# Even attention: a fourth probability buffer, paired ratios, scores three units ahead and issued later in the iteration

## The reference, cut to what matters

```python
def diff_attend(q, k, v, lam):
    s = jnp.einsum('bqhmd,bkhmd->bhmqk', q, k).astype(jnp.float32) * (A_QK ** -0.5)
    p = jax.nn.softmax(s, axis=-1)
    a = p[:, :, 0] - lam * p[:, :, 1]
    return jnp.einsum('bhqk,bkhd->bqhd', a, v.astype(jnp.float32))
```

## Time and profile before

| what | us |
|---|---|
| median of 3 runs | 2271.23 (2267.19 to 2271.67) |
| the profiled execution | 2276.89 |
| its span in the profile | 2275.2 |
| PE busy | 2193.6 (96% of the span) |
| DVE busy | 1353.2 (59%) |
| ACT busy | 557.7 (25%) |
| mean granted TensorE clock | 0.976 of full |

### The profile page before, as it was taken

How to read it: one execution, slowest core, us unless ns; L and a number is a source line. 1 busy time by engine, 2 the same in 40 slices (tenths; PEclk the granted TensorE clock), 3 DMA queues, 4 the chain that set the end, 5 groups by cost and what they waited for, 6 DMA issues and landing times.

```text
span 2275.2 us, 28228 instructions
## 1 busy us (share of the span) xinstructions
PE 2193.6 (96%) x11848; PEld 1785.6 (78%) x11848; DVE 1353.2 (59%) x1761; ACT 557.7 (25%) x1088; POOL 47.8 (2%) x31
## 2 busy tenths in 40 slices
PE   8999998889899999999999999999999999999998
PEld 5788885568788767777788888788888887888887
DVE  5123447985562374766697763464787536977733
ACT  3111015871231462364321110131100002211100
POOL 0000000000000020300000000000000000000000
PEclk8899999999799999999999999999999999999999
DMA  6232233221031112202222322322222222222322
GB/s 278 116 111 111 111 115 81 67 74 56 19 140 56 39 54 75 74 20 75 74 93 95 109 78 94 107 86 99 83 85 72 91 98 93 93 93 93 112 101 74
DMA packets 34238, 204.52 MB, mean 90 GB/s; under 512 B 4800, under 2 KB 5056, under 8 KB 14656
## 3 DMA queue, kind: packets, MB, share of 16 engines
q1 hardware_dynamic: 32736, 197.99, 25.0%
q10 hardware_dynamic: 1376, 4.72, 0.6%
HBM read 191.16 MB, written 2.10 MB: 85 GB/s over the span
## 4 chain that ended last, share of the span: by engine, by line
PE 87%; DVE 9%; ACT 2%; issue 1%; DMA 0%; DVEq 0%; SPq 0%; ACTq 0%
PE ps L412 23%; PE ps L413 22%; PE ps L414 22%; PE ps L518 3%; PE ps L519 3%; PE ps L520 3%; DVE stat L2110 2%; PE ps L633 2%; PE ps L567 1%; PE ps L550 1%; PE ps L1261 1%; PE ps L966 1%; PE ps L739 1%; PE ps L614 1%; PE ps L560 1%
## 5 line engine op out<-in xcount | busy, mean ns | idle before, releaser
L1833 DVE CAST whi<-raw 128x2048 fp32r<-128x2048 f32 (+2 forms) x148 | 172.0, 1162 | 448.4 <-DMA raw<-in_even 120.0
L412 PE MATMUL ps<-h2hi,whi 128*128 128x512 f32 (+1 forms) x1052 | 412.3, 392 | 2.6 <-DVE h2lo L1933 2.2
L413 PE MATMUL ps<-h2lo,whi 128*128 128x512 f32 (+1 forms) x1052 | 407.3, 387 | 0.0
L414 PE MATMUL ps<-h2hi,wlo 128*128 128x512 f32 (+1 forms) x1052 | 407.3, 387 | 0.0
L1834 DVE TENSOR_TENSOR wlo<-raw,whi 128x2048 fp32r<-128x2048 f32 (+2 forms) x148 | 320.1, 2163 | 5.1
L412 PE MATMUL ps<-h1hi,whi 128*128 128x512 f32 (+1 forms) x768 | 273.8, 356 | 5.4 <-DVE h1lo L1880 2.6
L413 PE MATMUL ps<-h1lo,whi 128*128 128x512 f32 (+1 forms) x768 | 269.5, 351 | 0.0
L414 PE MATMUL ps<-h1hi,wlo 128*128 128x512 f32 (+1 forms) x768 | 267.5, 348 | 0.0
L412 PEld LDWEIGHTS ps<-h2hi,whi 128*128 128x128 f32 x1052 | 197.8, 188 | 49.4 <-DVE h2lo L1933 8.3
L414 PEld LDWEIGHTS ps<-h2hi,wlo 128*128 128x128 f32 x1052 | 197.8, 188 | 40.5
L413 PEld LDWEIGHTS ps<-h2lo,whi 128*128 128x128 f32 x1052 | 197.9, 188 | 38.8
(11 more groups left out here) (323 smaller groups left out, 3350.8 us busy)
## 6 DMA issues: line engine op xcount, KB each, us to landing
raw<-in_ffn_in SPq DMA_DIRECT2D x44, 1024.0 KB, 4.9
raw<-in_even SPq DMA_DIRECT2D x16, 1024.0 KB, 7.6
mod_w<-in_mod SPq DMA_DIRECT2D x6, 2048.0 KB, 20.3
mraw<-in_mod SPq DMA_DIRECT2D x12, 1024.0 KB, 4.9
raw<-in_odd SPq DMA_DIRECT2D x12, 1024.0 KB, 4.9
raw<-in_sgu_v SPq DMA_DIRECT2D x12, 1024.0 KB, 4.8
raw<-in_sgu_u SPq DMA_DIRECT2D x12, 1024.0 KB, 4.9
raw<-in_sgu_out SPq DMA_DIRECT2D x16, 768.0 KB, 4.3
```

The source lines that it names most:

```text
L412: pe.matmul(o, r(lhi), r(rhi), start=first, stop=False, **kw)
L413: pe.matmul(o, r(lhi), r(rlo), start=False, stop=False, **kw)
L414: return pe.matmul(o, r(llo), r(rhi), start=False, stop=last, **kw)
L1833: step(dve.tensor_copy(whi[:, slot, 0:width].bitcast(F32R), raw[:, slot, 0:width]))
```

## The change

Two things are done at once. There are four probability buffers instead of three (two of them now lie where the last two tiles of h1hi and the first ones of h1lo will be written, so the last two convolved_parts get a wait for the transposes of unit 44). And the queues are shifted: PE issues the scores three units ahead, and no longer at the head of the iteration but behind the late transposes and the half of the products; ACT makes the exponentials two units ahead; DVE makes the maxima three units ahead and the ratios of two units (a = 0 and a = 1) together, 128 x 2 instead of twice 128 x 1, for which it waits for the exponentials of both. head_sums moves from (4, 0) to (3, 1), and head_variance from (4, 1) to (4, 0).

```diff
--- before.py
+++ after.py
@@ -167,7 +167,7 @@
         oept = [place(f"oept{i}", i * 4096, [12, P]) for i in range(2)]
         oprob = [place(f"oprob{i}", 8192 + i * 1536, [2, TA]) for i in range(3)]
         ept = [place(f"ept{i}", i * 768, [6, P]) for i in range(4)]
-        prob = [place(f"prob{i}", 6144 + i * 1536, [2, TA]) for i in range(2)]
+        prob = [place(f"prob{i}", at, [2, TA]) for i, at in enumerate((4608, 6144, 7680))]
         prob.append(temp[:, 0:2 * TA].rearrange("p (m n) -> p m n", m=2))
         oq, ok = place("oq", A0, [4, TX]), place("ok", A0 + 2048, [4, TA])
         ov = place("ov", A0 + 5120, [6, 512])
@@ -779,7 +779,7 @@
                     pe.wait_ge(ea["copied"], n)
                 for i, kt in enumerate(kts):
                     at = kt * P if EVEN_UNITS[u][1] < 4 else (kt - 4) * P
-                    last = transposed(ps[:, 6, i * P:(i + 1) * P], prob[u % 3][:, 0, at:at + P])
+                    last = transposed(ps[:, 6, i * P:(i + 1) * P], prob[u % 4][:, 0, at:at + P])
                 last.then_inc(ea["transposed"], 1)
 
             def head_sums(t, sums):
@@ -794,16 +794,17 @@
             even_scores(0)
             even_scores(1)
             pe.wait_ge(mod_ready, 8)
+            even_scores(2)
             last_unit = len(EVEN_UNITS) - 1
             for u, (hp, t, a) in enumerate(EVEN_UNITS):
-                if u < last_unit - 1:
-                    even_scores(u + 2)
-                if (t, a) == (4, 0) and hp:
-                    head_sums(hp - 1, head_sums_at(hp - 1))
                 if u:
                     even_transposes(u - 1, range(4, 6), moved[u] - 1)
                 if u >= 3:
                     even_pv((u - 3) // 2, (u - 3) % 2)
+                if u + 3 <= last_unit:
+                    even_scores(u + 3)
+                if (t, a) == (3, 1) and hp:
+                    head_sums(hp - 1, head_sums_at(hp - 1))
                 pe.wait_ge(ea["probs"], u + 1)
                 if t < 4:
                     even_transposes(u, range(4), moved[u])
@@ -1459,12 +1460,12 @@
                 t, b = EVEN_UNITS[u][1], 3 * (u % 2)
                 if m == 0:
                     act.wait_ge(ea["negmax"], u + 1)
-                    if u >= 3:
-                        act.wait_ge(ea["transposed"], moved[u - 2])
+                    if u >= 4:
+                        act.wait_ge(ea["transposed"], moved[u - 3])
                 flat = ps[:, b:b + 3, :].rearrange("p b n -> p (b n)")
                 n = TA if t < 4 else TC
                 at = m * (TA if t < 4 else 512)
-                act.activation(prob[u % 3][:, m, 0:n], flat[:, at:at + n], ACT.Exp,
+                act.activation(prob[u % 4][:, m, 0:n], flat[:, at:at + n], ACT.Exp,
                                bias=stat[:, 2 * (u % 4) + m:2 * (u % 4) + m + 1],
                                accum_out=stat[:, 8 + u % 4:9 + u % 4] if m else stat[:, 32 + u:33 + u])\
                     .then_inc(ea["exp"], 1)
@@ -1485,18 +1486,19 @@
                 cols = (slice(0, TX), slice(TX, TA))[part]
                 tell(copy(eot[:, hp, cols], ps[:, 7, 0:(TX, TC)[part]]), ea["out"], 2 * hp + part + 1)
 
-            even_exp(0, 0)
-            even_exp(0, 1)
+            for u in range(2):
+                for m in range(2):
+                    even_exp(u, m)
             last_unit = len(EVEN_UNITS) - 1
             for u, (hp, t, a) in enumerate(EVEN_UNITS):
                 if u and EVEN_UNITS[u - 1][1] < 4:
                     even_copy(u - 1, 0)
-                if u < last_unit:
-                    even_exp(u + 1, 0)
+                if u + 2 <= last_unit:
+                    even_exp(u + 2, 0)
                 if u:
                     even_copy(u - 1, 1)
-                if u < last_unit:
-                    even_exp(u + 1, 1)
+                if u + 2 <= last_unit:
+                    even_exp(u + 2, 1)
                 if (t, a) == (0, 0) and hp < 3:
                     even_hi(hp + 1)
                 if (t, a) == (1, 0) and hp:
@@ -2124,28 +2126,29 @@
             def convolved_parts(hp):
                 split_tensor(h1hi, h1lo, np.s_[:, 4 + hp, :], eob[:, hp, :], ea["mixed"], hp + 1)
 
-            even_max(0)
-            even_max(1)
+            for u in range(3):
+                even_max(u)
             for u, (hp, t, a) in enumerate(EVEN_UNITS):
                 n = TA if t < 4 else TC
                 i = u % 4
-                dve.wait_ge(ea["exp"], 2 * u + 2)
-                step(dve.reciprocal(stat[:, 12 + i:13 + i], stat[:, 8 + i:9 + i]))
-                step(dve.scalar_tensor_tensor(out=stat[:, 16 + i:17 + i], in0=stat[:, 32 + u:33 + u], scalar=lam4[:, 3:4],
-                                              in1=stat[:, 12 + i:13 + i], op0=ALU.mult, op1=ALU.mult))
-                p = prob[u % 3]
+                if (t, a) == (4, 0) and hp:
+                    head_variance(hp - 1)
+                if a == 0:
+                    dve.wait_ge(ea["exp"], 2 * u + 4)
+                    step(dve.reciprocal(stat[:, 12 + i:14 + i], stat[:, 8 + i:10 + i]))
+                    step(dve.scalar_tensor_tensor(out=stat[:, 16 + i:18 + i], in0=stat[:, 32 + u:34 + u], scalar=lam4[:, 3:4],
+                                                  in1=stat[:, 12 + i:14 + i], op0=ALU.mult, op1=ALU.mult))
+                p = prob[u % 4]
                 dve.scalar_tensor_tensor(out=p[:, 0, 0:n], in0=p[:, 1, 0:n], scalar=stat[:, 16 + i:17 + i],
                                          in1=p[:, 0, 0:n], op0=ALU.mult, op1=ALU.add).then_inc(ea["probs"], 1)
-                if u + 2 < len(EVEN_UNITS):
-                    even_max(u + 2)
+                if u + 3 < len(EVEN_UNITS):
+                    even_max(u + 3)
                 if (t, a) == (0, 1) and hp < 3:
                     even_lo(hp + 1)
-                if (t, a) == (4, 1):
-                    if hp:
-                        head_variance(hp - 1)
-                    if hp < 2:
-                        convolved_parts(hp)
-
+                if (t, a) == (4, 1) and hp < 2:
+                    convolved_parts(hp)
+
+            dve.wait_ge(ea["transposed"], moved[45])
             convolved_parts(2)
             convolved_parts(3)
             gated_head(0)
```

## The result

| | before | changed |
|---|---|---|
| median, us | 2271.23 (2267.19 to 2275.46, 5 runs) | 2321.28 (2310.43 to 2325.51, 5 runs) |
| span of the profiled execution | 2275.2 | 2308.7 |
| the stage: first scores to first matmul of the projection | 146.20 | 186.48 |
| granted clock in the stage | 0.92 | 0.75 |

The ratio is 1.0219, with a 95% interval of 1.0202 to 1.0236: 50 us slower.

The account below looks back on a forecast made before the run. DVE was taken to set the pace, 3.04 us a full unit, PE close behind at 2.75. At full clock +22.8 us, plus 5 for the low clock, made +28: 2271 + 28 = 2299 us, range 2279 to 2325.

Parts of the forecast that it names:

- A: The forecast case: the copy between early and late transposes is on PE's path, +15 to +45, 2286 to 2316; chance 0.62.
- B: Rival: PE's new gaps keep it at 1.2 GHz in most full units, +81, 2352 us; chance 0.10.
- The main sign: Late transposes in full units idle 0.6 to 0.8 us for the 128x512 copy, some 20 us total.
- the clock step: PE in the attention stage: three more iterations at 1.2 GHz, about one a border, 1.8 us each, +5.
- The copy on the path: PE, full units: late transposes wait for ACT's early copy; 3.51 us a unit for 3.04, 15.0 us over 32.
- DVE's new floor: DVE, full units: paired ratios lower its need from 3.04 to 2.82 us, 10.6 us over the stage.
- The place of the scores: PE, scores of u + 3: their wait for the exponentials of u + 1 costs nothing in the steady stretch.
- The borders: Head-pair borders: a pair takes 41.7 us for 36.6; 1.4 of the 5.1 more are the border.
- my walk: Three queues followed through twelve units at full clock: middle +16.2, start +4.0, tail +2.6, together +22.8 us.
- C: Rival: the copy falls into PE's slack and DVE's saving shows, -10.6, 2261 us; break-even gap 0.29; chance 0.09.
- D: Rival: the wait is there, but the third unit ahead heals the borders, +6, 2277 us; chance 0.15.

Follow-up runs that it names:

- The kernel with the scores first: Changed kernel with the scores of u + 3 back at the head of PE's iteration, between early and late transposes: 2274.84 us, ratio to before 1.0015.
- the one with the order alone: Kernel before with only scores (of u + 2) and head_sums moved behind the late transposes and products; three buffers, single ratios: 2305.17 us, ratio 1.0137.
- with the copy covered by products: Changed kernel with the half of the products before the late transposes, scores still behind both: 2287.11 us, ratio to before 1.0068.
- the filled gap: Changed kernel with six useless 512-column matmuls between early and late transposes of a full unit: 2301.6 us, ratio to before 1.0127.
- the second profile: Changed kernel profiled once more, nothing changed: 2322.63 us, 12.2 more than in the first profile.

## Why the prediction was right, and where its size was off

*The size.* The measured 2321.28 us lies in the stated range of 2279 to 2325, but 5 us above the band of A (2286 to 2316), toward B: +50 for +28. The main sign held: the late transposes wait for the 128x512 copy in all 32 full units, and these are 3.52 us apart. Most sizes were too small. That wait is 33.1 us (27.7 in PE's own rows) and not some 20, the stage 186 to 198 us and not 165 to 175, and DVE is idle a third of it and not a fifth. And the sign that was named against the clock step, a granted clock under 0.8 in the stage, came: 0.75 and 0.70.

*The copy on the path.* Right, almost to the hundredth: 1.35 us from early to late transposes and 3.51 us a full unit were forecast, 1.35 and 3.52 measured. The idle time is the forecast one too, if it is read where it was reckoned: 0.69 us of the PE row in each such unit (3.52 less 2.83 busy); the 0.93 to 0.96 in the PEld rows counts from the end of the weight loads. It was the sum of four rows with no choice in it. The kernel with the scores first and the one with the order alone show that this is the cause of most of the loss and not a companion. The Trainium skill's rule on rotating banks ("Perfetto Trace Analysis", "Optimizing Tensor Performance"), that the evacuation of one group should overlap the next group's matmuls, was borne out: the earlier trace rows had the price, and the 32 waits above are that copy each time.

*DVE's new floor.* 2.82 us a unit did not set the pace in the changed kernel, as forecast. That the price of the pairing lies in the wait for the second unit's exponentials shows where the depth is missing, 3.2 us a pair; with the depth it could not be told from nothing.

*The place of the scores.* I had put its cost at nothing, since the exponentials are long done when they are issued. That was half of it. Scores issued late also make the maximum late: with the copy covered by products, DVE waits 20 us more for scores than with the scores first, and the stage is 14 us longer, part of which can be the products' own waits. Behind the copy it did not show in my walk, because the walk charged the whole delay to the copy.

*The borders.* The walk starts from the fourth unit of a pair, (1, 1); the "(3, 0)" that it names for the 123.5 us is a slip. Its three parts and their measures in the first profile are the start, +6.8 us for +4.0; the middle, 136.05 us where 123.5 was forecast and 107.34 it was before, +28.7 for +16.2; and the tail, +4.8 for +2.6. Together they are the 40.3 for 22.8. The forecast of 41.7 us a head pair was for full clock; the second pair took 470.86 - 423.06 = 47.8 us between the same late transposes. Its long steps stand mostly where the walk had them: that for the difference behind convolved_parts, for example, forecast 4.4 us (17.7 to 22.1), is

```profile
443.53 0.20 PEld L633 LDWEIGHTS ps<-mats,prob 128*128 128x128 f32 x2
447.89 0.20 PEld L633 LDWEIGHTS ps<-mats,prob 128*128 128x128 f32 x2 [2.33 <-DVE prob L2142]
```

4.36 us, at full clock. One long step was too dear: 24.2 to 30.0, that is 5.8, measured 4.86, and at the low clock. How much of the rest is clock is not separated by a run for the border alone.

*The clock.* This is the term that was mis-sized. The forecast has "three such iterations, about one a border, +5, near the low end". There are 93 to 119 us at the low clock in the stage, against 23 before; the filled gap puts its cost at about 20 us, and the second profile adds 12 from the same source. The price of one low iteration was about right (5.3 forecast; 5.37 measured, and 5.48 and 5.49 for those that are low throughout); their number was not. The step that failed was the argument from the earlier trace rows, that a PE busy 0.76 of the time keeps the full clock. It failed in both directions. The clock did not only fall behind idle borders: of its nine falls in the first profile's stage, at 435.8, 483.5 and 527.9 it fell at the end of a row of full units in which PE never idled longer than 0.69 us at a time and had just been busy 88% of the time. In front of the first of these falls:

```profile
429.87:435.80 5.93, 5.24 (x52) 4.06 (x53) 3.31 (x5) 3.15 (x11) 0.00 (x0) 1.00 0.23 54
```

Among this work are the twelve 2-column matmuls of head_sums, 1.53 us that the change moved there; with the gaps filled and head_sums in the same place, PE is busy throughout and the clock does not fall in any of the three. Whether the 0.69 us gaps or head_sums decide is not separated. And once the clock had fallen, iterations of 5.5 us, in which PE was busy 88% of the time, did not bring it back, and how long it stayed low differed from one execution to the next.

What the term should have been is an estimate. As the rest over the walk's 22.8, it is 17.5 us in the first profile (40.3 - 22.8) and 29 in the second (52.1 - 22.8). From the low time, 70 and 96 us more than before times 0.36 (5.49 against 3.52 us for one iteration), it is 25 and 34, and then the part at full clock is 15 to 18 and the walk was 5 to 8 us too dear. No run decides between the two, but by either the forecast +5 was too small by 12 us or more. That the sum came within the range owes something to the width of the range. Case B, low in most full units, was thus half true, and I had it at 0.10 as all or nothing.

The Trainium skill's rule on transposes ("TensorE: Matmul & The Clock Gate", "Part 4: PE-mode transpose"), that they do not count for the clock as matmuls do, is not decided: all kernels here have the same transposes, and clocks from 0.70 to 0.93; what was added in the filled gap were matmuls, and the clock rose.

*The rivals.* C needed a gap under 0.29 us; it is 0.76 (1.35 - 0.59). D had the borders healed by the third unit ahead; with the scores first, where nothing hides it, the depth gives nothing (1.0015, 1.0027 with single ratios).

## What to carry to other kernels

Before an instruction group is moved down an in-order queue, look at which two groups become neighbours: if they share a bank, the copy between them is now on the queue's path, at its whole duration, once per iteration. Deeper look-ahead and more buffers do not help against it. And when a change takes the bound from another engine to PE, price its iterations at the low clock too, for as many as follow each fall of the clock, and not only for the one in which it fell: partly hidden before, they now cost their full length.

## What the runs showed of the hardware that was not expected

The low clock lasts. In the two low iterations above PE was busy 9.60 of 10.97 us, 88%, and stayed at 1.2 GHz (the same work takes longer there: 4.80 us of the first 5.49 for a unit's 26 matmuls, 2.83 at 2.4 GHz, and both units idle 0.69); in a full unit of the same stage at 2.4 GHz it was busy less, 2.83 of 3.52, 80%, and stayed there:

```profile
379.24:382.76 3.52, 2.83 (x26) 1.96 (x26) 3.08 (x5) 2.75 (x6) 0.00 (x0) 1.00 0.39 91
```

That row is of the changed kernel's first profile. So the busy share alone doesn't tell the level, nor does an idle border have to come before a fall: the clock also fell behind 5.93 us in which PE was busy 5.24. The same program took 2310 and 2322 us in its two profiled executions, with 93 and 119 us at the low clock. 192 useless matmuls made a kernel 20 us faster.
